# Expert weights in two-slot transfers, router logits with tokens on partitions, and a gather in fp32

## The reference

```python
D_MODEL = 1024; N_EXPERTS = 32; TOP_K = 4; D_FF = D_MODEL
def rms_norm(x, g):
    xf = x.astype(jnp.float32)
    y = xf * lax.rsqrt(jnp.mean(xf * xf, axis=-1, keepdims=True) + EPS)
    return (y * g.astype(jnp.float32)).astype(x.dtype)

def moe_ffn(h, w_router, b_router, w1, b1, w2, b2):      # h = rms_norm(x, norm_ffn_g)
    logits = (t @ w_router + b_router).astype(jnp.float32)
    top_v, top_e = lax.top_k(logits, TOP_K)
    gates = jax.nn.softmax(top_v, axis=-1)
    ...
    def expert_block(args):
        hh = xb @ w1[e] + b1[e]
        glu, lin = jnp.split(hh, 2, axis=-1)
        glu = jnp.minimum(glu, SWIGLU_LIMIT)
        lin = jnp.clip(lin, -SWIGLU_LIMIT, SWIGLU_LIMIT)
        act = glu * jax.nn.sigmoid(SWIGLU_ALPHA * glu) * (lin + 1.0)
        return act @ w2[e] + b2[e]
    y = segment_sum(out * row_gate, row_tok)             # x += y, then a final rms_norm
```

## Time and profile before

| what | us |
|---|---|
| median of 3 runs | 1312.46 (1311.49 to 1313.07) |
| the profiled execution | 1314.39 |
| its span on the core | 1312.7 |
| PE busy (91% of the span) | 1197.4 |
| DVE busy (31%) | 404.3 |
| ACT busy (17%) | 228.8 |
| POOL busy (4%) | 56.6 |
| DMA queue of SP, share of 16 engines | 87.3% |

### The profile page before, as it was taken

How to read it: one execution, slowest core, us unless ns; L and a number is a source line. 1 busy time by engine, 2 the same in 40 slices (tenths; PEclk the granted TensorE clock), 3 DMA queues, 4 the chain that set the end, 5 groups by cost and what they waited for, 6 DMA issues and landing times.

```text
span 1312.7 us, 17381 instructions
## 1 busy us (share of the span) xinstructions
PE 1197.4 (91%) x6756; PEld 593.6 (45%) x6756; DVE 404.3 (31%) x815; ACT 228.8 (17%) x356; POOL 56.6 (4%) x81
## 2 busy tenths in 40 slices
PE   7999999879499999999999998999989999989995
PEld 5778899657243443433433232323333232323231
DVE  3555667526712222121321212120312212121203
ACT  4332144312310111111111111101111011111012
POOL 5202001010300000000000000000000000000000
PEclk9999999989699999999999999999999999999998
DMA  9732289794599999999999999999999999999993
GB/s 314 250 120 83 97 262 309 253 380 163 232 373 418 418 417 417 417 417 417 419 418 418 418 417 419 417 417 417 417 417 419 418 418 418 418 418 418 417 417 119
DMA packets 123893, 467.06 MB, mean 356 GB/s; under 512 B 7440, under 2 KB 54064, under 8 KB 90864
## 3 DMA queue, kind: packets, MB, share of 16 engines
q1 hardware_dynamic: 116848, 455.37, 87.3%
q0 software_dynamic: 1616, 6.65, 1.6%
q10 hardware_dynamic: 5392, 4.54, 1.1%
HBM read 460.84 MB, written 5.70 MB: 355 GB/s over the span
## 4 chain that ended last, share of the span: by engine, by line
PE 49%; DMA 36%; SPq 9%; DVE 3%; issue 2%; ACT 1%; DVEq 0%; ACTq 0%
DMA ring<-w 34%; PE bank L1624 15%; PE bank L1276 9%; SPq L303 7%; PE bank L1656 6%; PE bank L1443 5%; PE bank L1600 4%; PE bank L1580 2%; PE bank L1431 2%; SPq L305 1%; DMA ring<-k_t 1%; DMA ring<-v_c 1%; PE bank L1643 1%; DMA ring<-w_in 1%; PE bank L1476 1%
## 5 line engine op out<-in xcount | busy, mean ns | idle before, releaser
L1624 PE MATMUL bank<-ring,rest 128*64 128x512 f32 x2048 | 463.6, 596 | 29.8 <-DMA ring<-w 27.5
L1624 PEld LDWEIGHTS bank<-ring,rest 128*64 128x64 f32 x2048 | 139.4, 136 | 333.9 <-issue 234.7
L1656 PE MATMUL bank<-ring,rest 128*64 128x512 f32 x1024 | 226.8, 595 | 16.4 <-ACT rest L731 16.4
L1212 DVE TENSOR_SCALAR rest<-bank 128x512 f32<-128x512 f32 x32 | 22.1, 691 | 521.7 <-PE bank L1624 521.7
L1656 PEld LDWEIGHTS bank<-ring,rest 128*64 128x64 f32 x1024 | 70.8, 137 | 151.8 <-issue 127.8
L1191 DVE TENSOR_TENSOR rest<-rest,bank 128x512 f32<-128x512 f32 (+1 forms) x102 | 66.9, 680 | 227.6 <-PE bank L1600 227.5
L1276 PE MATMUL bank<-rest,ring 128*128 128x288 f32 (+1 forms) x512 | 124.6, 403 | 8.7 <-DMA ring<-w_in 8.7
L1276 PEld LDWEIGHTS bank<-rest,ring 128*128 128x128 f32 x512 | 97.7, 192 | 33.1 <-DMA ring<-w_in 8.7
L727 ACT ACTIVATE rest<-rest 128x512 f32<-128x512 f32 x32 | 20.2, 630 | 520.7 <-DVE rest L1212 520.7
L1600 PE MATMUL bank<-rest 128*128 128x512 f32 (+1 forms) x204 | 98.4, 611 | 1.3 <-ACT rest L739 1.3
L1443 PE MATMUL bank<-split 128*128 128x288 f32 x576 | 81.2, 302 | 2.0 <-DVE split L1058 1.8
(11 more groups left out here) (297 smaller groups left out, 699.8 us busy)
## 6 DMA issues: line engine op xcount, KB each, us to landing
ring<-w SPq DMA_DIRECT2D x384, 1024.0 KB, 21.8
ring<-w_in SPq DMA_DIRECT2D x12, 1024.0 KB, 12.0
ring<-k_t SPq DMA_DIRECT2D x8, 1024.0 KB, 6.2
ring<-v_c SPq DMA_DIRECT2D x8, 1024.0 KB, 13.1
ring<-w_xk SPq DMA_DIRECT2D x4, 1024.0 KB, 5.0
ring<-w_xv SPq DMA_DIRECT2D x4, 1024.0 KB, 5.0
ring<-w_out SPq DMA_DIRECT2D x4, 1024.0 KB, 6.6
ring<-w_xq SPq DMA_DIRECT2D x4, 1024.0 KB, 6.2
```

The source lines that it names most:

```text
L1624: last = t.matmul(out, slots[:, k, :], w[:, col], start=False, stop=(k == KT - 1))
L1656: last = t.matmul(ps[2][CAP * ds:CAP * ds + CAP, :], actT[:, a * P + CAP * cg:a * P + CAP * cg + CAP], w[:, cg, 512 * ds:512 * ds + 512], ...
```

## The change

**Transfers.** `load_expert_units` fills two neighbouring slots with one DMA of 2 MB. Partition p takes two consecutive rows of w1 (16 KB in one piece) or four consecutive rows of w2 (also 16 KB). SP waits until both slots have been used, PE waits for the first slot's semaphore at every second unit. As the rows of a partition are now neighbours, the contraction is numbered differently: the gather picks every second feature column (`cols_d`), the transposes of the activations every fourth (`act[:, a:512:4]`). Slot 15 is no longer filled early.

**Router.** PE computes the logits with tokens on partitions, three matmuls for each k, into banks 5 to 7 (`L_BANK`). ACT squares x feature-major (`sq_r`), POOL adds tiles 1 to 6, PE sums over features with a column of ones; ACT takes the roots of three columns. DVE replaces the four largest logits by a marker (`match_replace`) and compares with the original for `chosen`; padding replaces the `valid` mask. The gates are a masked softmax over 32 columns.

**Gather.** ACT writes fp32 token rows scaled by 1/rms (`h_rows`), half from `y` and half straight from the banks; no bf16 parts. The gather is 24 fp32 matmuls. The norm's gain is applied when the gathered features leave the banks: ACT four passes for bank 4, DVE one for bank 5. `select_pair` is one instruction. POOL, not DVE, clears `outp[1]`.

```diff
-        def load_expert_unit(eng, e, j):
+        def load_expert_units(eng, e, j):
             s, q = (j + PRE) % SLOTS, j % EXP_UNITS
             e = e + j // EXP_UNITS
+            both = cells(s * SLOT, (s + 2) * SLOT)
             if q < W1_UNITS:
-                return eng.dma_start(slot[s], w1[e, q * P:(q + 1) * P, :]).then_inc(ring_in[s], 16)
...
+                src = w1[e, q * P:(q + 2) * P, :].rearrange("(p r) c -> p (r c)", r=2)
+            else:
+                src = w2[e, (q - W1_UNITS) * 256:(q - W1_UNITS + 2) * 256, :].rearrange("(p r) c -> p (r c)", r=4)
+            return eng.dma_start(both, src).then_inc(ring_in[s], 16)
...
-                    for j in range(HELD + 4, SLOTS - PRE):
-                        load_expert_unit(sp, 0, j)
...
+                for j in range(first, BODY * EXP_UNITS, 2):
+                    sp.wait_ge(units_used, g * (BODY * EXP_UNITS) + j + 1 - SLOTS + 1)
+                    load_expert_units(sp, i * BODY, j)
...
+            wait_unit_used(sp, U_XO + 2)
+            load_expert_units(sp, 0, 0)
+            wait_unit_used(sp, U_XO + 3)
+            for j in range(2, SLOTS - PRE, 2):
+                load_expert_units(sp, 0, j)
...
+            for k in range(1, KT - 1):
+                pool.wait_ge(rsq_done, k + 1)
...
+                pool.tensor_tensor(sq_r[:, 0, :], sq_r[:, 0, :], sq_r[:, k, :], ALU.add).then_inc(rsq_sum, 1)
+            pool.wait_ge(proj, 64)
+            pool.memset(outp[1], 0.0).then_inc(outp_done, 2)
...
             for tt in range(TT):
+                R = ROWS[tt]
+                a.activation(h_rows[0:R, tt, 0:512], y[0:R, tt, 0:512], ACT.Copy, scale=yrs[0:R, tt:tt + 1])
...
             def evac_gather(nth, parity):
-                q = xg[parity].rearrange("p k s -> p (k s)")
                 act_e.wait_ge(xg_ps, 2 * nth - 1)
-                a.copy(q[:, 0:512], ps[4][:, :]).then_inc(xg_done, 1)
-                act_e.wait_ge(xg_ps, 2 * nth)
-                a.copy(q[:, 512:1024], ps[5][:, :]).then_inc(xg_done, 1)
+                for k in range(KT // 2):
+                    last = a.activation(xg[parity][:, k, :], ps[4][:, k * P:(k + 1) * P], ACT.Copy, scale=gain_k[:, k:k + 1])
+                last.then_inc(xg_done_a, 1)
...
+            def evac_gather(nth, parity):
+                dve.wait_ge(xg_ps, 2 * nth)
+                v.tensor_tensor(xg[parity][:, KT // 2:KT, :], ps[5][:, :].rearrange("p (k s) -> p k s", s=P),
+                                gain_k[:, KT // 2:KT].unsqueeze(2).to_broadcast([P, KT // 2, P]),
+                                ALU.mult).then_inc(xg_done_v, 1)
...
+                    if j % 2 == 0:
+                        evac_gather(g * (BODY // 2) + j // 2 + 2, (j // 2 + 1) % 2)
...
             def gather():
                 for d in range(KT):
+                    cols_d = slice(256 * (d // 2) + d % 2, 256 * (d // 2) + 256, 2)
                     for tt in range(TT):
-                        for s in range(3):
-                            last = t.matmul(ps[4 + d // 4][:, (d % 4) * P:(d % 4 + 1) * P],
-                                            hx[:, s, tt, d * P:(d + 1) * P], sel[:, tt, :],
-                                            start=(tt == 0 and s == 0), stop=(tt == TT - 1 and s == 2))
+                        R = ROWS[tt]
+                        last = t.matmul(ps[4 + d // 4][:, (d % 4) * P:(d % 4 + 1) * P],
+                                        h_rows[0:R, tt, cols_d], sel[0:R, tt, :], start=(tt == 0), stop=(tt == TT - 1))
...
-                        pe.wait_ge(xg_done, g * BODY + 2 * (j // 2 + 2))
+                        pe.wait_ge(xg_done_a, g * (BODY // 2) + j // 2 + 2)
                     for a in range(4):
-                        last = t.transpose(ps[4][:, a * P:(a + 1) * P], act[:, a * P:(a + 1) * P], ident)
+                        last = t.transpose(ps[4][:, a * P:(a + 1) * P], act[:, a:512:4], ident)
```

More of the change, by code:

```diff
@@ L1077, in split_bias, with x_rows @@
                     v.memset(selGT, 0.0).then_inc(selgt_zero, 1)
-            def x_rows(half):
-                for tt in range(TT):
-                    dve.wait_ge(y_ps, TT * half + tt + 1)
+            def x_rows(pieces):
+                for n in pieces:
+                    half, tt = n // TT, n % TT
+                    dve.wait_ge(y_ps, n + 1)
+                    if half:
+                        dve.wait_ge(h_ready, tt + 1)
                     v.tensor_copy(y[0:ROWS[tt], tt, 512 * half:512 * half + 512],
-                                  ps[Y_BANK[TT * half + tt]][0:ROWS[tt], :]).then_inc(y_ev, 1)
+                                  ps[Y_BANK[n]][0:ROWS[tt], :]).then_inc(y_ev, 1)
             for c in range(KT):
@@ L1533, in router, with x_rows @@
                 pe.wait_ge(x_add, KT + k + 1)
-                return t.matmul(ps[6][0:NE, 0:T], wr[:, k, :], xT[:, k, :], start=(k == 0), stop=(k == KT - 1))
-            def x_rows(half):
                 for tt in range(TT):
-                    R, n = ROWS[tt], TT * half + tt
-                    if n > TT:
-                        pe.wait_ge(y_ev, n - TT)
+                    R = ROWS[tt]
+                    last = t.matmul(ps[L_BANK[tt]][0:R, 0:NE], xT[:, k, tt * P:tt * P + R], wr[:, k, :],
+                                    start=(k == 0), stop=(k == KT - 1))
+                return last
+            def x_rows(pieces):
+                for n in pieces:
+                    half, tt = n // TT, n % TT
+                    R = ROWS[tt]
+                    if n in (2, 5):
+                        pe.wait_ge(y_ev, 1 if n == 2 else TT)
                     for k in range(4):
@@ L1553, in _ @@
                 if c == 5:
-                    x_rows(0)
+                    x_rows(range(2))
+                if c == 6:
+                    x_rows(range(2, TT))
             router(KT - 2)
-            router(KT - 1).then_inc(lg_ps, 1)
-            x_rows(1)
-            pe.wait_ge(lg_done, 1)
-            pe.wait_ge(y_ev, TT)
+            router(KT - 1)
+            pe.wait_ge(rsq_done, KT)
+            pe.wait_ge(rsq_sum, KT - 2)
             for tt in range(TT):
                 R = ROWS[tt]
-                last = t.transpose(ps[5][0:R, tt * NE:(tt + 1) * NE], std[0:NE, tt * P:tt * P + R], ident[0:NE, 0:NE])
-            last.then_inc(lt_ps, 1)
+                for k in (0, KT - 1):
+                    last = t.matmul(ps[L_BANK[tt]][0:R, NE:NE + 1], sq_r[:, k, tt * P:tt * P + R], ones[:, 0:1],
+                                    start=(k == 0), stop=(k == KT - 1))
+            last.then_inc(rss_ps, 1)
+            x_rows(range(TT, 2 * TT))
             pe.wait_ge(chosen_done, 1)
@@ L1586, in _ @@
             pe.wait_ge(sel_done, 1)
-            pe.wait_ge(h_split, 3)
+            pe.wait_ge(h_ready, TT)
+            gather()
             pe.wait_ge(y_ev, 2 * TT)
-            gather()
             pe.wait_ge(gates_done, 1)
@@ L1652, in turn @@
                     for a in range(W2_UNITS):
-                        w = expert_unit(W1_UNITS + a).rearrange("p (h c) -> p h c", h=2)
-                        for cg in range(2):
+                        w = expert_unit(W1_UNITS + a).rearrange("p (r c) -> p r c", r=2)
+                        cg = a // 2
+                        for b in range(2):
                             for ds in range(2):
-                                last = t.matmul(ps[2][CAP * ds:CAP * ds + CAP, :],
-                                                actT[:, a * P + CAP * cg:a * P + CAP * cg + CAP],
-                                                w[:, cg, 512 * ds:512 * ds + 512], start=(a == 0 and cg == 0),
-                                                stop=(a == W2_UNITS - 1 and cg == 1))
+                                at = (2 * (a % 2) + b) * P + CAP * cg
+                                last = t.matmul(ps[2][CAP * ds:CAP * ds + CAP, :], actT[:, at:at + CAP],
+                                                w[:, b, 512 * ds:512 * ds + 512], start=(a == 0 and b == 0),
+                                                stop=(a == W2_UNITS - 1 and b == 1))
                         last.then_inc(units_used, 1)
```

213 lines of the change are left out of this document (88 added, 125 removed).

## The result

The changed kernel takes 1328.38 us (median of four, 1327.73 to 1330.52) against 1312.70 us; the runs of the two compared give a ratio of 1.0124, 95% interval 1.0106 to 1.0141. It is slower by 15.7 us where 1285 was forecast, outside the range of 1276 to 1302.

The account below looks back on a forecast made before the run. Weight transfers were taken to set the pace after the router: stream back at 366.3, 180 transfers of 4.95 us to 1257.3, plus 26.4 and 1.8, a span of 1285.5; median forecast 1285 us, range 1276 to 1302.

Parts of the forecast that it names:

- the price of the gather: Gather of 24 fp32 matmuls: 48 records at 0.108 us, 5.2 to 5.5 us, taken as 5.3.
- the forecast pair (56.2): Expert loop: PE needs 56.2 us for a pair of experts, with the gather at 5.3 for 4.19.
- the overlap: Expert loop: PE's 56.2 us a pair stays hidden under the transfers' 59.4; PE may reach 57.9 before setting the end.
- Rival 2: PE becomes the bound through strided reads in gather and activations; doubled load time gives 1342 us; chance 0.12, 0.09 slower.
- the break-even: Gather in the loop: each microsecond beyond 7.0 us costs 16; at 8.7 us the change's gain is gone.
- The start: Router up to the first expert matmul: taken at 338 us, 17 us earlier than 354.92.
- The unit of 2.475 us: Weight stream: a unit in 16 KB rows takes 2.475 us, a transfer 4.95, a full pair 59.4.
- the prediction's own sum: Weight stream: back at 366.3, 180 transfers of 4.95 us, then 26.4 and 1.8 us to the end: 1285.5.
- Rivals 1 and 3: Long weight rows no faster: 1292 to 1298 us, chance 0.20; or slower: 1312 or 1337 us, chance 0.06.
- rival 4: Router shortens by half only, ACT's rows or bias load taking over: start at 346, 1293 us; chance 0.07.
- the wait for ACT's second copy: Expert loop: PE's pair loses the 0.68 us in which its transposes waited for ACT's second copy.

Follow-up runs that it names:

- 128-row run: Changed kernel with its gather reading all 128 rows of the third token tile, stride of two kept; 1276.60 us, 0.9715 of the kernel before.
- both edits: Changed kernel with a 128-row gather and contiguous gather columns, w1 in 8 KB pieces, w2 still in 16 KB rows; 1285.68 us.
- one-slot transfers: New router and 128-row gather, with expert weights in the 1 MB transfers and old layout of the kernel before; 1297.98 us.
- old pieces: Changed kernel with 128-row gather and 2 MB transfers, but w1 in 8 KB and w2 in 4 KB pieces, without the strides; 1300.57 us.
- the one with 3 switches: Changed kernel with the 32-row matmuls put together behind the 128-row ones in each half of the gather, stride kept; 1280.54 us.
- the bf16 run above: Kernel before, its bf16 gather reading only 32 rows of the third token tile; 1329.06 us against 1312.71 beside it.
- transfers alone: Kernel before with its own router and bf16 gather, given only two-slot transfers with 16 KB rows and their layout; 1294.34 us.

## Why the prediction was wrong

**The step that failed is the price of the gather.** It said 48 records at 0.108 us, from a row whose matmuls all have 128 rows. That price holds for such a stream: with 128 rows and contiguous columns the gather took 5.55 us, 0.116 a record. But the code that the prediction read gives `h_rows[0:R]`, with R = 32 in every third matmul, and that row has no such matmul in it. The difference between the forecast pair (56.2) and the measured one (59.88) adds up from the runs: 15 switches of 0.193 make 2.90, one more into the transposes 0.21, the stride 0.30, and the 48 records without either 0.25 (5.55 for 5.3): 3.66 of 3.68. With it fell the overlap: 59.88 us is more than the 58.73 that the transfers need for a pair, so TensorE, which the prediction hid under them, set the end.

**Rival 2 had the outcome and the wrong mechanism.** It put the break-even at a gather of 8.7 us, and 8.75 came; "pairs are equally long from first to last without DMA waits" is what the trace shows. Most of the loss beyond break-even is the start, 8 us late, and some 0.3 us a pair, mostly the switch into the transposes. Yet the rival blamed the stride, which is 0.30 us a gather; that its figure was met is luck. For the activations' stride of four, too, the runs show little: the four transposes of an odd expert take 0.76 us with the stride and 0.67 without (128-row runs with 16 KB and with 4 KB pieces), those of an even one 0.48 and 0.45, 0.12 us a pair. The Trainium skill (SBUF — State Buffer, "Door 1: The DMA port swizzle") had been read as 0.9 us a pair; the trace does not bear that out. What the Trainium skill has against the change, the drain at a change of tiling mode (TensorEngine Tiling (Array Packing), "Key Properties"), the prediction did not use.

**The start.** Reciprocal, ACT's rows, the select and the gather's start were each forecast within 0.6 us. The first expert matmul, "at 337.5, or 340 if the clock has fallen" and taken as 338, came at 346.08; the first gather's 13.47 us for 5.3 are all of that. With 128 rows it stood at 338.28, behind a gather of 5.89 us from 331.68. The first gather of the changed kernel is also longer than its 8.75 us in the loop, and that goes with the granted clock; windows of the changed kernel, then of the 128-row run (columns as in the earlier trace rows):

```profile
330.00:334.00 4.00, 2.92 (x15) 2.47 (x16) 3.77 (x12) 2.50 (x4) 0.00 (x0) 0.90 0.96 391
334.00:338.00 4.00, 4.00 (x15) 3.01 (x13) 0.43 (x2) 0.85 (x4) 0.00 (x0) 0.50 1.03 438
338.00:346.00 8.00, 8.00 (x28) 5.46 (x29) 1.24 (x5) 0.94 (x4) 0.00 (x0) 0.50 0.93 396
346.00:350.00 4.00, 4.00 (x12) 1.16 (x10) 1.89 (x7) 1.10 (x1) 0.00 (x0) 0.50 0.01 4
```

```profile
330.00:334.00 4.00, 2.71 (x29) 2.65 (x30) 3.33 (x11) 3.10 (x5) 0.00 (x0) 1.00 0.98 378
334.00:338.00 4.00, 4.00 (x36) 3.73 (x36) 1.24 (x6) 1.21 (x5) 0.00 (x0) 1.00 1.00 426
```

From 334 us on TensorE is busy throughout in both, at 0.50 until 350 in the one, at 1.00 in the other. The first gathers without switches took 5.89, 5.60, 8.40 and 7.83 us (128 rows, both edits, one-slot transfers, old pieces), the one with 3 switches 8.45, and the clock was back at 1.00 by 338 in all five; with 8 or 15 switches they took 11.85, 13.47 and 14.14, and it was not. That goes with the switches and with the bf16 run above, but that the switches hold the clock down is not shown: no run changed the clock alone.

**The unit of 2.475 us was too long, not too short.** 58.73 / 24 is 2.447. The prediction split the pair of 60.23 with one w1 interval, found 5.5 ns fixed per packet and warned that 5 ns of error in that interval would move the unit. The three pair times do without it: 58.73 us with 16 KB rows alone, 59.36 with w1 in 8 KB (16 x 4 packets per engine more, 9.8 ns each), 60.25 with w2 in 4 KB besides (8 x 12 more, 9.3 ns each). With 2.447 the prediction's own sum reads 366.3 + 180 x 4.894 + 28.2 = 1275.4; the 128-row run has a span of 1276.3, and its stream, at 172 GB/s from 366 to 368 us, is back at 397 behind that. So the step by which it forecast the stream was right for a gather without switches, and its unit was 0.03 us too long. (The steady 417 to 419 GB/s of the earlier trace rows begin in the thirteenth slice, not the twelfth; nothing hangs on it.)

**The sum of the parts.** Against 1312.9 us, transfers alone give 1294.3, the router alone (128-row gather) 1298.0, both 1276.6: 18.6 and 14.9 apart, 36.3 together. Rivals 1 and 3 (longer rows no faster, or slower) and rival 4 (half the router) have fallen with it. In the loop the wait for ACT's second copy, 0.68 us in the earlier trace rows, went as said.

## What to carry over

Take a matmul's price from a row that has its shape and its neighbours' shape: here a stream that mixed operands of 32 or 64 rows with 128 paid at every change, padding to 128 rows (or 96) cost nothing, and putting the short matmuls together saved most of it. The padding rows have to hold zeros in one operand and finite data in the other. When a change frees the resource that sets the pace, work out how much the next one has left, here 1.7 us a pair, and look hardest at what the change adds on that engine. Several runs with different piece sizes give a fixed cost per packet; one interval does not.

## What was not expected of the hardware

- A change between 128-row and 32- or 64-row operands cost 0.193 to 0.198 us in fp32 and 0.103 us (32 rows) in bf16; 128 to 96 cost nothing.
- The fixed cost of a packet in this stream was 9.3 to 9.8 ns (pairs of 58.73, 59.36 and 60.25 us), so that rows of 16 KB ran at 428 GB/s and the old mix at 418.
- The granted clock fell to 0.50 behind the bf16 gather with switches inside the loop: 9.67 us for w2 matmuls that take 7.09. Why only in this run, and only in some pairs, stays open.
